# A two-layer streaming encoder on one core: the experts' weights move from the scatter's placement to the copied rows, and the scatter becomes two rounded products per block

## The reference, cut to what matters

```python
logits = (xf @ w_router) + b_router
top_logit, top_idx = lax.top_k(logits, 2)
top_w = softmax(top_logit)
# each expert e computes, for the tokens that chose it,
out = (silu(xb @ w1[e]) * (xb @ w3[e])) @ w2[e]        # 1024 -> 3584 -> 1024
# and the result is summed back to the tokens, scaled by the token's weight for this expert
y = zeros((n_tok, 1024)).at[row_tok].add(out * row_w[:, None])
```

## Time and profile before

| | |
|---|---|
| time, median of 3 runs | 1807.88 us (1806.66 to 1808.66) |
| the profiled execution | 1806.65 us, span 1804.6 us |
| mean granted clock of TensorE | 0.974 |
| TensorE busy | 1683.0 us (93% of the span) |
| VectorE busy | 1386.7 us (77%) |
| ScalarE busy | 1022.1 us (57%) |
| weights read | 500.5 MB, mean 278 GB/s |

### The profile page before, as it was taken

The page is one execution under the profiler, slowest core; times in us unless marked ns, Lnnn a source line. Parts: engine busy times, 40 slices in busy tenths (PEclk is TensorE's granted clock), DMA queues, the critical chain, the costliest instruction groups (busy, mean ns, idle before and its releaser), DMA issues.

```text
span 1804.6 us, 21121 instructions
## 1 busy us (share of the span) xinstructions
PE 1683.0 (93%) x7472; PEld 1310.4 (73%) x7473; DVE 1386.7 (77%) x1187; ACT 1022.1 (57%) x815; POOL 36.8 (2%) x40
## 2 busy tenths in 40 slices
PE   1999899999999979989999989999999999999995
PEld 0587758887777757768877778887777777887773
DVE  7686868666786878878878956656689788787887
ACT  0475433432565237767767755554577776776772
POOL 1100010000100000000000000000000000000000
PEclk9999999999999979999999989999999999999998
DMA  9895459764875348989979966666599899899991
GB/s 343 320 320 164 162 180 339 274 233 140 287 251 192 129 146 301 389 303 364 366 255 369 385 222 217 221 214 230 194 379 387 299 380 373 306 373 332 330 391 72
DMA packets 210534, 502.31 MB, mean 278 GB/s; under 512 B 9137, under 2 KB 13409, under 8 KB 210481
## 3 DMA queue, kind: packets, MB, share of 16 engines
q1 hardware_dynamic: 208770, 496.15, 76.7%
q0 software_dynamic: 1712, 5.43, 1.0%
HBM read 500.50 MB, written 1.05 MB: 278 GB/s over the span
## 4 chain that ended last, share of the span: by engine, by line
PE 81%; DVE 11%; issue 6%; ACT 1%; DMA 1%; POOL 0%; DVEq 0%; SPq 0%; ACTq 0%; POOLq 0%
PE ps L1395 21%; PE ps L1397 20%; PE ps L1396 20%; DVE w_lo L1270 4%; PE ps L1406 4%; PE ps L1401 3%; PE ps L1402 3%; PE ps L1937 2%; PE ps L1822 2%; PE ps L1862 1%; DVE mod_acc L884 1%; DVE w_lo L859 1%; DVE gates L1072 1%; DVE stats L906 1%; PE ps L1520 1%
## 5 line engine op out<-in xcount | busy, mean ns | idle before, releaser
L1270 DVE TENSOR_TENSOR w_lo<-w_raw,w_hi 128x2048 fp32r<-128x2048 f32 x333 | 757.6, 2289 | 214.0 <-ACT w_hi L740 211.9
L740 ACT CAST w_hi<-w_raw 128x2048 fp32r<-128x2048 f32 x333 | 634.4, 1909 | 236.2 <-PE ps L1397 148.7
L1395 PE MATMUL ps<-w_hi,actT_hi 128*128 128x512 f32 (+1 forms) x1464 | 582.9, 398 | 30.5 <-DVE w_lo L1270 16.6
L1397 PE MATMUL ps<-w_hi,actT_lo 128*128 128x512 f32 (+1 forms) x1464 | 568.0, 388 | 0.0
L1396 PE MATMUL ps<-w_lo,actT_hi 128*128 128x512 f32 (+1 forms) x1464 | 567.6, 388 | 0.0
L1395 PEld LDWEIGHTS ps<-w_hi,actT_hi 128*128 128x128 f32 x1464 | 277.4, 189 | 103.6 <-DVE w_lo L1270 27.7
L1397 PEld LDWEIGHTS ps<-w_hi,actT_lo 128*128 128x128 f32 x1464 | 277.3, 189 | 57.4
L1396 PEld LDWEIGHTS ps<-w_lo,actT_hi 128*128 128x128 f32 x1464 | 277.7, 190 | 54.4 <-issue 2.4
L859 DVE TENSOR_TENSOR w_lo<-w_raw,w_hi 128x2048 fp32r<-128x2048 f32 x81 | 185.4, 2290 | 91.6 <-ACT w_hi L488 91.4
L488 ACT CAST w_hi<-w_raw 128x2048 fp32r<-128x2048 f32 x81 | 154.5, 1908 | 114.4 <-PE ps L1397 99.6
L1401 PE MATMUL ps<-w_hi,gT_hi 128*128 128x512 f32 x336 | 140.8, 419 | 14.7 <-DVE gT_hi L1297 14.7
(11 more groups left out here) (240 smaller groups left out, 1230.0 us busy)
## 6 DMA issues: line engine op xcount, KB each, us to landing
w_raw<-in_exp_w_dram SPq DMA_DIRECT2D x336, 1024.0 KB, 6.4
w_raw<-in_ffn_w_dram SPq DMA_DIRECT2D x33, 1024.0 KB, 5.3
w_raw<-in_w_mod_mix_dram SPq DMA_DIRECT2D x24, 1024.0 KB, 8.6
w_raw<-in_w_mod_ffn_dram SPq DMA_DIRECT2D x24, 1024.0 KB, 6.2
w_raw<-in_w_gate_dram SPq DMA_DIRECT2D x24, 1024.0 KB, 6.4
w_raw<-in_w_in_dram SPq DMA_DIRECT2D x14, 1024.0 KB, 8.1
w_raw<-in_w_out_dram SPq DMA_DIRECT2D x8, 1024.0 KB, 5.1
w_raw<-in_w_branch_c_dram SPq DMA_DIRECT2D x4, 1024.0 KB, 5.1
```

Source lines behind the costliest of these rows:

```text
L740: nc.scalar.copy(w_hi[:, i % SPLIT, :], w_raw[:, i % RING, :]).then_inc(split_hi, 1)
L1270: TTn(w_lo[:, i % SPLIT, :], w_raw[:, i % RING, :], w_hi[:, i % SPLIT, :].bitcast(F32), ALU.subtract).then_inc(piece_used, 1)
L1395: MM(to, hi, w_h, start=first, stop=False)
L1397: return MM(to, lo, w_h, start=False, stop=last)
```

## The change

The scatter's placement no longer carries the weights: it is the turned `pick`, zeros and ones, which the rounded form holds exactly, so `place` is `F32R`. The weights go to the slots by a product of their own: `pick` by a column `w_token` of the tokens' weights, into bank 1, from where ScalarE copies them to `w_slot`, one number for a slot. `pick_w` is gone; VectorE copies the column `w_token` in its place. At the end of an expert ScalarE copies the whole width of y scaled by `w_slot` and rounded to `y_hi`; VectorE then computes `y` times `w_slot` less `y_hi` into `y_lo`, over the whole width, and waits for ScalarE's copy. The scatter is `place` by `y_hi` plus `place` by `y_lo`: eight rounded products for a block. `y_hi` lies over `hbuf`, `y_lo` over `mod_acc`, both free in this stage.

```diff
-        hbuf = sb("hbuf", [P, TT, D])
+        pair = ExitStack()
+        hbuf = sb("hbuf", [P, TT, D], scope=pair)
+        pair.close()
+        y_hi = sb("y_hi", [P, 2, D], F32R)
...
+        w_token = sb("w_token", [P, TT, 1])
+        w_slot = sb("w_slot", [P, 2])
...
-        place = sb("place", [P, 2, SEQ], scope=ffn)
+        place = sb("place", [P, 2, SEQ], F32R, scope=ffn)
...
                                 act.wait_ge(place_sent, e + 1)
+                                A(w_slot[:, 0:blocks], ps[:, 1, 0:blocks], ACT.Copy)
                                 ins = A(place[:, 0:blocks, :], ps[:, 0, 0:blocks * SEQ].rearrange("p (b q) -> p b q", q=SEQ), ACT.Copy)
...
                                     act.wait_ge(place_copied, e + 1)
+                                    A(w_slot[HALF_P:P, half:half + 1], ps[0:HALF_P, 1, half:half + 1], ACT.Copy)
...
-                                    ins = A(hbuf[:, b, 0:BANK], bank(2 * b), ACT.Copy)
+                                    ins = A(y_hi[:, b, :], ps[:, 2 * b:2 * b + 2, :].rearrange("p c q -> p (c q)"), ACT.Copy,
+                                            scale=w_slot[:, b:b + 1])
...
-                            at = posm[:, t, bass.ds(e, 1)]
-                            TS(pick[:, t, :], iota, at, None, ALU.is_equal)
-                            ins = TS(pick_w[:, t, :], iota, at, wsel[:, t, bass.ds(e, 1)], ALU.is_equal, ALU.mult)
-                        ins.then_inc(pick_ready, 1)
+                            TS(pick[:, t, :], iota, posm[:, t, bass.ds(e, 1)], None, ALU.is_equal)
+                        nc.vector.tensor_copy(w_token[:, :, :], wsel[:, :, bass.ds(e, 1)]).then_inc(pick_ready, 1)
...
                                 dve.wait_ge(split_used, done0 + (EXPERT.n_split + SPLIT))
+                                dve.wait_ge(y_act, e + 1)
                                 for b in range(blocks):
-                                    ins = nc.vector.tensor_copy(hbuf[:, b, BANK:D], bank(2 * b + 1))
+                                    ins = STT(y_lo[:, b, :], ps[:, 2 * b:2 * b + 2, :].rearrange("p c q -> p (c q)"), w_slot[:, b:b + 1],
+                                              y_hi[:, b, :].bitcast(F32), ALU.mult, ALU.subtract)
...
                                     for t in range(TT):
-                                        ins = TR(ps[:, 0, b * SEQ + t * P:b * SEQ + (t + 1) * P], pick_w[:, t, b * P:(b + 1) * P], ident)
+                                        MM(ps[:, 1, b:b + 1], pick[:, t, b * P:(b + 1) * P].bitcast(F32), w_token[:, t, :], start=t == 0, stop=t == TT - 1)
+                                    for t in range(TT):
+                                        ins = TR(ps[:, 0, b * SEQ + t * P:b * SEQ + (t + 1) * P], pick[:, t, b * P:(b + 1) * P].bitcast(F32), ident)
...
-                                        ins = MM(bank(2 * t + c), place[:, b, t * P:(t + 1) * P], hbuf[:, b, c * BANK:(c + 1) * BANK],
-                                                 start=b == 0, stop=b == blocks - 1)
+                                        to, cols = place[:, b, t * P:(t + 1) * P], slice(c * BANK, (c + 1) * BANK)
+                                        MM(bank(2 * t + c), to, y_hi[:, b, cols], start=b == 0, stop=False)
+                                        ins = MM(bank(2 * t + c), to, y_lo[:, b, cols], start=False, stop=b == blocks - 1)
```

More of the change, by code:

```diff
@@ L221, in trunk @@
         cst = sb("cst", [P, CONSTS])
-        mod_acc = sb("mod_acc", [P, 3 * D])
+        pair = ExitStack()
+        mod_acc = sb("mod_acc", [P, 3 * D], scope=pair)
+        pair.close()
+        y_lo = sb("y_lo", [P, 2, D], F32R)
+        sb("mod_acc_rest", [P, D])
+        w_token = sb("w_token", [P, TT, 1])
+        w_slot = sb("w_slot", [P, 2])
         gate1 = sb("gate1", [P, D])
@@ L265, in trunk @@
         pick = sb("pick", [P, TT, SEQ], F32R, scope=ffn)
-        pick_w = sb("pick_w", [P, TT, SEQ], scope=ffn)
-        place = sb("place", [P, 2, SEQ], scope=ffn)
+        place = sb("place", [P, 2, SEQ], F32R, scope=ffn)
         zeros = sb("zeros", [P, BANK], F32R, scope=ffn)
```

## The result

| | before | changed |
|---|---|---|
| median of 7 runs | 1806.66 us (1802.11 to 1808.66) | 1820.39 us (1813.47 to 1822.94) |
| ratio to before, 95% interval | | 1.0078 [1.0064, 1.0091] |
| profiled execution, its span | 1806.65, 1804.6 | 1817.7, 1815.9 |
| mean granted clock | 0.974 | 0.970 |

The account below looks back on a forecast made before the run. TensorE was taken as the bound, 81% of the chain, with tails ended by VectorE's cast. Tails -0.1, weight products +3.96 and picking -0.45 made +3.4 us: 1811.3 us from a median of 1807.88, range 1805.5 to 1816.5.

Parts of the forecast that it names:

- in the others the gather passed at full clock: TensorE's gathers: only the second tail's stretch at clock 0.50 followed a gap and the gather, costing 3 us.
- the products that carry the weights: Placement, first panel of each expert: 18 unrounded 128x1 products at 0.22 us, all on the path, +3.96 us.
- The tails: From an expert's last product to the next one's first; eight of them, together -0.1 us.
- the scatter's saving is waited away: End of each expert: 14.8 us less TensorE work, worth only what the next product waits for the scatter.
- the cast sets the end: Tail's new end: VectorE's cast of gathered rows, 0.60 us later, plus 1.43, or the shorter scatter, whichever is later.
- The second's -1.8: Second tail, scatter at half clock: next expert's second product at 933.8 against 935.57, cast ending well ahead.
- The eighth tail: End of last expert: nothing hides ScalarE's and VectorE's longer copies; adds follow 0.59 apart instead of 0.86; +0.55 us.
- The picking: VectorE's picking of tokens: two of four instructions go, one tiny copy comes; -0.45 us before the loop, nothing inside.
- The rival of the clock: More TensorE idle time in tails adds half-clock stretches: one makes 1814.3 us, two 1817; 22 in 100.
- a scatter that is waited for: Rival, tails: next product waits for the scatter, so its whole saving comes out, 1796.6 us; 7 in 100.
- rounded products that run no faster: Rival, scatter: rounded products with a freshly written placement take 0.43 us like unrounded records, about 1815.8 us; 5 in 100.
- the middle's shares: Chances of a result within 0.2%: 28 from the forecast's case, 14 cheap weight products, 3 the clock's; given as 46.

Follow-up runs that it names:

- a_pad32: Changed kernel with 16 never-executed products put ahead of TensorE's expert loop to shift its code; 1810.83 us, ratio 1.0035 to the kernel before.
- a_pad96: Changed kernel with 48 never-executed products put ahead of TensorE's expert loop; 1810.54 us, ratio 1.0030 to the kernel before.
- the swap: Changed kernel, code shifted by 16 or 48 never-executed products, VectorE's cast of gathered rows ahead of the next piece's split; 1795.89 or 1797.95 us.
- b_pad96: Kernel before with 48 never-executed products put ahead of TensorE's expert loop; 1804.83 us, ratio 0.9995.
- a_swap: Changed kernel, TensorE's code not shifted, with VectorE's cast of gathered rows ahead of the next piece's split; 1814.09 us, ratio 1.0052 to the kernel before.
- a_pad10: Changed kernel with 2 never-executed products, some 10 instructions, ahead of TensorE's loop; 1823.63 us, ratio 1.0091 to the kernel before.
- b_pad48: Kernel before with 24 never-executed products, some 54 instructions, ahead of TensorE's expert loop; 1820.48 us, ratio 1.0083.

## Why the prediction was wrong

**The step that failed** is the one that let only executed instructions count on TensorE: "in the others the gather passed at full clock", and the sum that took the gather's length from before. The prediction priced the products that carry the weights by their running time, +3.96, and not by their place in the code, where they push everything behind them. That cost 8 us (a_pad32 and a_pad96 against the changed kernel), more than twice the whole forecast change of +3.4. The rows that could have told were there: idle time put down to "issue" right before the gathers, and transfers of instructions in the DMA view of a tail.

**The tails.** That the scatter's saving is waited away, and that the cast sets the end, was right; the swap shows it, since 0.7 to 0.9% appear as soon as the cast is moved. By size, with the border out of the gathers in both programs (b_pad96 to a_pad32, table above): fourth -1.03 against a forecast of -1.0; third +0.18 for +0.60; fifth, sixth and seventh +0.85, +1.24 and +0.52 for +0.60 each. The second's -1.8 hung on a stretch of half clock that these two executions don't have; there it is -0.42, and the first's +0.37 for -0.26.

In the fifth and sixth the stretch of half clock has moved from ahead of the tail to behind it, which lengthens the tail and shortens the panel. So count from the start of an expert's last down products to the next expert's: from the fifth expert to the sixth 124.88 us before and 126.11 in the changed kernel, then 129.35 and 130.51, then 126.61 and 127.64. That is +1.23, +1.16 and +1.03, and the forecast was 0.60 for the cast and 0.44 for the weight products, +1.04. For these experts it was right, and half clock cost next to nothing more.

The eighth tail of the changed kernel answers to the earlier trace rows. ScalarE's copy:

```profile
1792.82 1.11 ACT L836 ACTIVATE y_hi<-ps,w_slot 128x1024 fp32r<-128x1024 f32 x1 [7.94 <-PE ps L1413]
```

VectorE's instruction behind it, and the adds:

```profile
1794.05 1.28 DVE L1361 SCALAR_TENSOR_TENSOR y_lo<-ps,w_slot,y_hi 128x1024 fp32r<-128x1024 f32 x1 [6.89 <-ACT y_hi L836]
1796.22 2.48 DVE L1371 TENSOR_TENSOR yacc<-yacc,ps 128x512 f32<-128x512 f32 x4 [0.89 <-PE ps L1952]
```

And the first scatter product between them:

```profile
1795.48 0.47 PE L1951 MATMUL ps<-y_hi,place 128*128 128x512 f32 x1 [2.70 <-DVE y_lo L1361]
```

From ScalarE's start to the end of the adds 5.88 us, against 1787.39 - 1782.15 = 5.24: +0.64, forecast +0.55. The scaled copy took 1.11 and the adds followed 0.62 apart, as told.

**The products for the weights**: 0.40 for a block instead of 0.44, 3.6 us instead of 3.96. They neither vanished nor took 0.43 us each. **The picking** before the loop, VectorE of the changed kernel:

```profile
664.03 0.62 DVE L1255 TENSOR_SCALAR pick<-cst,posm 128x256 fp32r<-128x256 f32 x2
664.57 0.16 DVE L1256 COPY w_token<-wsel 128x2 f32<-128x2 f32 x1
664.63 4.49 DVE L870 TENSOR_TENSOR w_lo<-w_raw,w_hi 128x2048 fp32r<-128x2048 f32 x2
```

The split behind it starts 0.60 us after the first, where it was 1.18: -0.58, forecast -0.45.

Like for like this makes +1.7 in seven tails, +0.64 in the eighth, +3.6 and -0.6, together +5.3, beside 5.4 to 6.3 us by the ratios of the shifted versions. The agreement is partly luck: the two executions that gave the tails are only 1.2 us apart as a whole, and from the first tail's last product to the eighth's a_pad32 takes 3.8 us more than b_pad96, a_pad96 7.2 us more. So the priced part, +3.4, seems short by two or three, about what the intervals allow, and which term holds them is open.

**The rival of the clock** was the nearest of those named and is not the cause. Its idle times came, and experts six and seven begin at half clock; but the kernel before had as much half clock ahead of those tails, so more idle time did not only add such stretches. In the gathers of the first and fourth tails half clock comes behind the stop, and in a_pad32, without the stop, they pass at full clock. Windows of the changed kernel:

```profile
1055.00:1270.00 215.00, 209.17 (x972) 171.53 (x972) 127.30 (x96) 107.23 (x93) 0.00 (x0) 1.00 0.63 211
1270.00:1400.00 130.00, 123.05 (x543) 98.03 (x541) 102.94 (x63) 89.48 (x63) 0.00 (x0) 0.97 0.87 315
```

The granted clock is 1.00 over the third tail and the fourth expert, which have no stop, and 0.97 over the stretch with the fourth tail's; the same stretches of the kernel before read 0.98 and 0.99. So in the first of them the changed kernel had more clock, and in the second less, where the stop is. The rivals of a scatter that is waited for and of rounded products that run no faster are refuted by the fifth tail. (Two small slips in the prediction change nothing: the last rival's terms, 2.8 and 1.4 on top of 1811.3, make 1815.5 and not 1815.8, and the middle's shares of 28, 14 and 3 make 45 and not 46.)

## What to carry to other kernels

An instruction in a loop with branches can cost twice: its time, and its place in the code. Before blaming an edit, look for idle time put down to "issue" inside a run of products that waits for nothing, and shift the code by some instructions that are never executed; if the time moves by as much as you are looking for, it is the place. And when the work that ended second is made shorter, look for the cheapest way to let the last one end earlier: here the new scatter brought 0.4 to 0.5% under the kernel before only with two instructions of another engine exchanged (0.13% of it is the exchange's own) and with the code out of the border's way.

## What the runs showed of the hardware that was not expected

- TensorE stopped for 1.08 us (a_swap, fourth tail) to 3.5 us (a_pad10, first tail; b_pad48, fourth) in the middle of a run of products, at a fixed place in the code, in tails 1, 2 and 4 and never in 3 and 5 to 7, and went on 2.3 to 2.8 us after a transfer of 16 KB of instructions had started. In the changed kernel's fifth to seventh no block of instructions was fetched; whether it was still held from the expert before was not tried.
- Ten instructions more ahead of the loop moved the stop by four products (10 to 6); each is a load and a product.
- The same never-executed instructions in the kernel before cost 0.83% at one distance (54 instructions) and nothing at another (about 100).
- The stretch at half clock about the fifth and sixth tail stood ahead of the tail in the kernel before (0.50 from 1396.0 to 1398.5) and behind it in the changed one (0.59 from 1416.0 to 1419.0).
- An unrounded product of one column, two records, took 0.20 us, about as much as one of eight columns.
